# Later modulation units and passes, small rows ahead of x, and more scale columns on TensorE in a one-layer transformer kernel

## The reference

```python
mod = silu(c) @ w_ada + b_ada                       # (1024) @ (1024, 6*1024)
sh1, sc1, g1, sh2, sc2, g2 = split(mod, 6)
h = rmsnorm(x, pre_mix_gain) * (1 + sc1) + sh1
y = token_mixer(h, ...)                             # h @ w_in (1024 x 3072), 4 differential
                                                    # and 8 MoBA heads, @ w_out
x = x + g1 * rmsnorm(y, post_mix_gain)
h = rmsnorm(x, pre_ffn_gain) * (1 + sc2) + sh2
y = hier_moe(h, ...)                                # 32 SwiGLU experts, 2 per token
x = x + g2 * rmsnorm(y, post_ffn_gain)
```

## Time and profile before

| what | value |
|---|---|
| median of 3 runs | 747.18 us (745.7 to 748.9) |
| the profiled execution's own time | 747.51 us |
| its span in the profile | 745.8 us |
| PE busy | 713.7 us (96%) |
| DVE busy | 643.8 us (86%) |
| ACT busy | 523.9 us (70%) |
| POOL busy | 148.4 us (20%) |
| HBM read and written | 334 GB/s over the span |

### The profile page before, as it was taken

How to read it: one execution, slowest core, us unless ns; L and a number is a source line. 1 busy time by engine, 2 the same in 40 slices (tenths; PEclk the granted TensorE clock), 3 DMA queues, 4 the chain that set the end, 5 groups by cost and what they waited for, 6 DMA issues and landing times.

```text
span 745.8 us, 13100 instructions
## 1 busy us (share of the span) xinstructions
PE 713.7 (96%) x4839; PEld 567.5 (76%) x4839; DVE 643.8 (86%) x575; ACT 523.9 (70%) x571; POOL 148.4 (20%) x190
## 2 busy tenths in 40 slices
PE   4999799998899999999999999999999999999994
PEld 4785685545778888888888888888888888888873
DVE  4635776756779999999999999999999999999995
ACT  4011233644568888888888888888888888888883
POOL 5502100040141112221111122211111122111000
PEclk9999899999699999999999999999999999999998
DMA  8999998823398999999999999999999999999901
GB/s 304 347 379 391 386 403 343 314 83 145 137 322 311 380 382 377 381 383 375 375 377 374 386 368 384 383 378 371 380 374 382 383 377 380 377 382 377 356 1 60
DMA packets 102154, 249.20 MB, mean 334 GB/s; under 512 B 5266, under 2 KB 5326, under 8 KB 100078
## 3 DMA queue, kind: packets, MB, share of 16 engines
q1 hardware_dynamic: 99648, 244.33, 88.3%
q0 software_dynamic: 1008, 3.31, 1.2%
q10 hardware_dynamic: 1470, 1.22, 0.5%
HBM read 247.78 MB, written 1.07 MB: 334 GB/s over the span
## 4 chain that ended last, share of the span: by engine, by line
PE 90%; DVE 4%; DMA 3%; ACT 1%; issue 1%; ACTq 0%; DVEq 0%; SPq 0%
PE PS L1485 48%; PE PS L1473 8%; PE PS L1434 6%; PE PS L1191 4%; PE PS L1452 4%; PE PS L1443 4%; PE PS L1352 3%; PE PS L1235 3%; PE PS L1247 2%; DVE MOD L784 1%; DMA W<-in_w_in_dram 1%; DMA PT<-in_pre_mix_gain_dram 1%; DMA W<-in_w_ada_dram 1%; PE PS L1146 1%; PE PS L1264 1%
## 5 line engine op out<-in xcount | busy, mean ns | idle before, releaser
L1033 DVE TENSOR_TENSOR WL<-W,WH 128x2048 fp32r<-128x2048 f32 x185 | 417.5, 2296 | 9.1 <-ACT WH L688 9.1
L688 ACT CAST WH<-W 128x2048 fp32r<-128x2048 f32 x185 | 346.6, 1907 | 0.0
L1485 PE MATMUL PS<-WH,XT 128*128 128x512 f32 x512 | 142.5, 400 | 1.4 <-DVE XT L1052 1.4
L1485 PE MATMUL PS<-WL,XT 128*128 128x512 f32 x508 | 138.2, 393 | 0.0
L1485 PEld LDWEIGHTS PS<-WL,XT 128*128 128x128 f32 x508 | 95.3, 188 | 22.4
L1485 PEld LDWEIGHTS PS<-WH,XT 128*128 128x128 f32 x512 | 93.7, 188 | 21.3 <-DVE XT L1052 1.5
L457 POOL COPY cur<-PG 128x2 f32 (+1 forms) x31 | 5.7, 184 | 369.7 <-PE PS L1463 369.4
L1485 PE MATMUL PS<-WH,HT 128*128 128x512 f32 x248 | 69.6, 402 | 1.6 <-DVE HT L1064 1.6
L1485 PE MATMUL PS<-WL,HT 128*128 128x512 f32 x248 | 67.7, 395 | 0.0
L469 POOL CAST cur<-PG 128x6 bf16 (+1 forms) x31 | 58.5, 1887 | 0.0
L1485 PEld LDWEIGHTS PS<-WH,HT 128*128 128x128 f32 x248 | 44.3, 188 | 16.4 <-issue 8.0
(11 more groups left out here) (227 smaller groups left out, 887.4 us busy)
## 6 DMA issues: line engine op xcount, KB each, us to landing
W<-in_w_gate_dram SPq DMA_DIRECT2D x64, 1024.0 KB, 8.1
W<-in_w_down_dram SPq DMA_DIRECT2D x64, 1024.0 KB, 6.3
W<-in_w_up_dram SPq DMA_DIRECT2D x63, 1024.0 KB, 9.5
W<-in_w_ada_dram SPq DMA_DIRECT2D x16, 1024.0 KB, 7.7
W<-in_w_in_dram SPq DMA_DIRECT2D x12, 1024.0 KB, 8.4
W<-in_w_ada_dram SPq DMA_DIRECT2D x16, 512.0 KB, 5.8
W<-in_w_out_dram SPq DMA_DIRECT2D x4, 1024.0 KB, 8.0
toe<-line_dram POOLq DMA_DIRECT2D x1, 1536.0 KB, 12.2
```

The lines of the kernel that those rows point to most:

```text
L688: nc.scalar.copy(WH[(UPE * odd + u) % SPLITS][:], source).then_inc(hi_ready, 1)
L1033: nc.vector.tensor_tensor(low, source, WH[(UPE * odd + u) % SPLITS][:].bitcast(f32), ALU.subtract).then_inc(lo_ready, 1)
L1485: last = nc.tensor.matmul(PS[:, bank, :], lhsT, w[:, q * 512:(q + 1) * 512], start=begin, stop=end)
```

## The change

Six edits. (1) The order of the units: 3, 2, 3 and 8 `ada` units stand between and behind the `win` pairs in place of 4, 3, 4 and 5, so each `win` pair comes earlier; the `wout` units come in the order 2, 3, 0, 1. (2) DVE runs passes 0 and 1 ahead of the lambda sums and 2 and 3 behind them, instead of six passes behind them; then one pass in each of g = 0 to 3, two in each of g = 4 to 6, one in g = 7 and one behind. (3) ACT issues the small rows of gain, scale and shift ahead of x. (4) ON_TENSOR has four rows, k = 6, 7 too, so DVE has two passes fewer and PE 16 records more. (5) The shift columns go to two PSUM banks, two columns each; ACT copies one pair for itself, DVE the other; the two clears stand behind `shift_columns(0)`. (6) POOL's gain and router loads wait for w_in's unit (5, 1), and `sum_part(4)` and `sum_part(5)` each stand behind one more `project_out`.

```diff
-    between = (4, 3, 4, 5)
+    between = (3, 2, 3, 8)
...
-    return units + [("wout", u, 0) for u in range(4)]
+    return units + [("wout", u, 0) for u in (2, 3, 0, 1)]
...
-        ON_TENSOR = (2, 3)
-        FIRST_DONE = {(1, 0): 2, (1, 1): 6, (0, 0): 10, (0, 1): 15, (1, 2): 19, (1, 3): 23, (0, 2): 27, (0, 3): 32}
+        ON_TENSOR = (2, 3, 6, 7)
+        FIRST_DONE = {(1, 0): 2, (1, 1): 4, (0, 0): 8, (0, 1): 13, (1, 2): 17, (1, 3): 21, (0, 2): 25, (0, 3): 30}
...
-            pool.wait_ge(unit_in[slot_of(UNIT_AT["win", 3, 1])], 16 * uses_of(UNIT_AT["win", 3, 1]))
+            pool.wait_ge(unit_in[slot_of(UNIT_AT["win", 5, 1])], 16 * uses_of(UNIT_AT["win", 5, 1]))
...
                 act.dma_start(cR, c.rearrange("b (k p) -> (b k) p", p=P)).then_inc(c_in, 16)
-                for t in range(TT):
-                    act.dma_start(X[:, t, :], x[0, t * P:(t + 1) * P, :]).then_inc(x_in[t], 16)
                 act.dma_start(gainR, pre_mix_gain.rearrange("b (k p) -> (b k) p", p=P)).then_inc(pre_gain_in, 16)
                 act.dma_start(scaleR, b_ada[:, D:2 * D].rearrange("b (k p) -> (b k) p", p=P)).then_inc(ada_b_in, 16)
                 act.dma_start(shiftR, b_ada[:, 0:D].rearrange("b (k p) -> (b k) p", p=P)).then_inc(ada_b_in, 16)
+                for t in range(TT):
+                    act.dma_start(X[:, t, :], x[0, t * P:(t + 1) * P, :]).then_inc(x_in[t], 16)
...
                 act.wait_ge(scale_ready, half + 1)
+                act.wait_ge(shift_mm, 2 * half + 1)
+                nc.scalar.copy(shcol[:, 4 * half:4 * half + 2], PS[:, 3, 0:2]).then_inc(shift_ready, 1)
                 act.wait_ge(shift_ready, half + 1)
...
-                dve.wait_ge(shift_mm, half + 1)
-                nc.vector.tensor_copy(shcol[:, four], PS[:, 3, 0:4]).then_inc(shift_ready, 1)
                 dve.wait_ge(xT_mm, 2 * TT)
-                dve.wait_ge(shift_ready, half + 1)
+                dve.wait_ge(shift_mm, 2 * half + 2)
+                link(nc.vector.tensor_copy(shcol[:, 4 * half + 2:4 * half + 4], PS[:, 2, 0:2]))
...
+            dve.wait_ge(ada_b_rest, 16)
+            for n in range(2):
+                ada(n)
             dve.wait_ge(lam_in, 64)
...
-            dve.wait_ge(ada_b_rest, 16)
-            for n in range(6):
+            for n in range(2, 4):
                 ada(n)
...
             for g in range(PAIRS):
                 scores(g)
-                ada(6 + g)
+                ada(4 + g + max(g - 4, 0))
+                if 4 <= g < PAIRS - 1:
+                    ada(5 + g + (g - 4))
                 probabilities(g)
-            ada(14)
             ada(15)
...
-                    at = UNIT_AT["first", 1, 0]
-                    pe.wait_ge(unit_in[at], 16)
                     for k in ON_TENSOR:
+                        at = UNIT_AT["first", 1, k // 4]
+                        pe.wait_ge(unit_in[at], 16)
...
-                nc.tensor.matmul(PS[:, 3, 0:4], shiftR, ident[0:DC, 4 * half:4 * half + 4], start=True, stop=True)
+                for chunk in range(2):
+                    at = 4 * half + 2 * chunk
+                    nc.tensor.matmul(PS[:, 3 - chunk, 0:2], shiftR, ident[0:DC, at:at + 2], start=True, stop=True)
                 for chunk in range(2):
                     pe.wait_ge(first_used, FIRST_DONE[0, 2 * half + 1] - 1 + chunk)
-                    for col in (2 * chunk, 2 * chunk + 1):
-                        last = add_rows(PS[:, 3, col:col + 1], 0, 4 * half + col)
-                last.then_inc(shift_mm, 1)
+                    for col in range(2):
+                        last = add_rows(PS[:, 3 - chunk, col:col + 1], 0, 4 * half + 2 * chunk + col)
+                    last.then_inc(shift_mm, 1)
...
             scale_columns(0)
-            pe.wait_ge(bank_zero, 1)
-            pe.wait_ge(gcol_ready, 1)
-            clear(0)
-            clear(1)
             for t in range(TT):
...
             shift_columns(0)
+            pe.wait_ge(bank_zero, 1)
+            pe.wait_ge(gcol_ready, 1)
+            clear(0)
+            clear(1)
...
             transpose_probabilities(7)
-            sum_part(4)
             values_out(5)
             project_out(1, [5], False, False)
+            sum_part(4)
             weigh_values(7)
-            sum_part(5)
             values_out(6)
             project_out(1, [6], False, False)
+            sum_part(5)
             spread_inverse(0)
```

More of the change, by code:

```diff
@@ L1155, in scale_columns @@
                     pe.wait_ge(c_silu, 1)
-                    at = UNIT_AT["first", 1, 0]
-                    pe.wait_ge(unit_in[at], 16)
                     for k in ON_TENSOR:
+                        at = UNIT_AT["first", 1, k // 4]
+                        pe.wait_ge(unit_in[at], 16)
                         for col in range(4):
-                            nc.tensor.matmul(PS[:, 2, col:col + 1], W[at][:, k * HALF + col * P:k * HALF + (col + 1) * P], cS[:, k:k + 1],
+                            nc.tensor.matmul(PS[:, 2, col:col + 1], W[at][:, k % 4 * HALF + col * P:k % 4 * HALF + (col + 1) * P], cS[:, k:k + 1],
                                              start=False, stop=True, skip_group_check=True)
```

## The result

The changed kernel's median is 740.92 us (740.76 to 742.1, 5 runs), beside 745.7 us (744.43 to 748.9, 5 runs) of the kernel before on the same chip: ratio 0.9935, 95% interval 0.9908 to 0.9962. Timed again beside other runs of the kernel before it had 740.33 us, ratio 0.9914 (0.9893 to 0.9935). That is 4.8 and 6.9 us. Of the 2 us, 1.5 are not the change: beside the changed kernel the kernel before has 745.7 us, and the forecast started from its 747.18. The gain itself was forecast at 4.3 us. The profiled execution took 740.76 us with a span of 739.0 us (before 747.51 and 745.8 us).

A forecast was written before the change was run, and what follows sets the result against it. The expert stage was taken as fixed, so time ahead of it counts fully. A 5.3 us lead, start's +0.6 included, less 1.0 given back makes -4.3: 747.51 to 743.2, median 0.33 lower, 742.9 us; range 740.4 to 746.0.

The forecast's parts named there:

- What bounds the kernel: Expert stage: PE full, fixed time from the first gather, so time gained ahead moves the end one for one.
- The first scores and the clock: `scores(0)`, released by ACT's exponential, at 75.2 not 78.15 us (-3.0); PE's stand falls from 4.15 to 0.6 us.
- The clock's part: Second projection round: no half clock without the long stand, 9.35 becomes 6.91 us, -2.4; rival, clock still falls, chance 0.12.
- Passes in pairs: DVE, g = 4 to 6: first pair covered with 0.14 us left; rival, PE stands for DVE, 749.5 us, chance 0.06.
- The copy behind `exps(7)`: `sum_part(3)` waits for ACT's copy until 137.4 us, giving back 1.0 of the 5.3 us lead.
- The start: Edits 3, 4, 5, up to 58 us: unit 1 lands no earlier, 16 new PE records cost time, +0.6 us (0 to 1.5).
- The rival of an earlier rise: Start: 16 more PE records raise the clock earlier, -2.3 us and no start loss, 740.0 us, chance 0.11.

The follow-up runs named there:

- once more: The changed kernel, nothing altered, timed and profiled again in the next group of runs: 740.33 us, ratio 0.9914.
- The two runs with the filled stand: Kernel before with 14 unread matmuls in PE's stand behind `score(1)`: 749.51 us; the same with POOL's gain and router loads late: 743.8 us.
- stand filled: Kernel before with 14 matmuls, result unread, put ahead of the first transposes of the probabilities, loads left early: 749.51 us, ratio 1.003.
- two scale rows: The changed kernel with ON_TENSOR back at (2, 3), edit 4 undone: 740.79 us, ratio 0.9913.
- all but the passes: The changed kernel with edit 2 undone, six DVE passes again behind the lambda sums: 750.25 us, ratio 1.0049.
- the start alone: The kernel before with edits 3, 4 and 5 only: 745.65 us, ratio 0.9979.

## Why the prediction was right, point by point

The times of PE in the table are those of the timeline; the chain has some of them 0.2 us later.

| step | forecast | changed kernel | once more |
|---|---|---|---|
| unit 1 landed | 12.95 us | 11.61 | 11.89 |
| `half_projection` starts | 25.7 us | 23.08 | 24.12 |
| projection 2 starts (57.98 before) | 58.6 us | 55.93 | 57.69 |
| first scores | 75.2 us | 72.56 | 74.32 |
| from projection 2 to the first scores | 16.6 us | 16.63 | 16.63 |
| stand of PE for the first probabilities | 0.6 us | 0.62 | 0.63 |
| second round | 6.9 us | 6.91 | 6.91 |
| `sum_part(3)` | 137.4 us | 134.43 | 136.21 |
| the 48 records | 152.5 us | 149.31 | 151.09 |

**What bounds the kernel: held.** PE is busy for all of the 100 us from 300 us on after the change as well, and SP stands for PE 170 times, 380.1 us. The time gained ahead of the experts came out at the end, 6.8 of 7.5 us in the profile.

**The first scores and the clock: held, the way from projection 2 to the scores to a tenth of a us.** The exponential releases the scores, in the changed kernel and with edit 2 alone. What was needed for it was edit 2. The clock's part went with the stand and was somewhat larger than forecast: PE's lead over the kernel before grows from 5.59 us at the first transposes (84.85 and 79.26) to 8.39 at the second (95.89 and 87.50), 2.8 us and not 2.4, since the first transposes had run at the lower level too (0.90 us, now 0.55). The changed kernel's second profile has 3.82 and 6.61 us, the same 2.8. The two runs with the filled stand show that this term holds only together with units that are in time. I had this as one sentence ("its unit lands earlier than before, since POOL's gain rows no longer run beside it"), and the 1.003 of the first of them is what it is worth when it fails. The reason in it was not what counted: with edit 2 alone POOL's loads stay early, and the pass of the second head pair, at 81.07 us, has no wait, because it is pass 5 there and not pass 7.

**Passes in pairs: held, with little room.** 0.14 us was forecast and 0.05 us measured at the fifth head pair. This rival did not come: the view of PE's waits shows no stand for DVE from the second head pair to the eighth.

**The copy behind `exps(7)`: held.** PE's lead is 8.33 us before `sum_part(3)`, where PE then stands 1.23 us, and 7.5 us at the 48 records. In between the kernel before had stood 0.39 us for its last pass at `sum_part(4)`, and the changed one doesn't. So 0.9 of 8.4 us were given back, where 1.0 was forecast; in the second profile 0.9 of 6.6.

**The start: the step that failed.** It was forecast at +0.6 us, from "x and the first units share the same transfers, so their order doesn't bring unit 1 earlier". Their order does: the eight profiles with the small rows first have unit 1 by 11.47 to 11.89 us, the six with x first by 12.01 to 12.97 us. Of the 1.6 us between the forecast 25.7 us and the 24.12 us of the second profile, 1.06 us are this. The cost of the 16 new records was right (3.57 us, forecast 3.50), and with x first the changed kernel does start late. What the start as a whole is worth is best read at projection 2 over all profiles: the five with the kernel before's start have 55.92, 55.93, 55.97, 55.98 and 57.98 us, the five with the changed start (not counting those with a part of it) 54.88, 55.92, 55.93, 55.99 and 57.69 us. The medians are 55.97 and 55.93 us. So the start's term is 0, not +0.6 us, and the profile that the forecast started from was the latest of its five there, by 2 us.

**The first scores were undersized by that late start.** In the kernel before, a lead at projection 2 does not reach the first scores whole, because they wait for the sixth pass's unit. From projection 2 to the first scores the kernel before took 20.2 us. With the stand filled, which is the same code up to there, it was 21.1 us (55.97 to 77.09), and with the small rows first 20.9 (56.35 to 77.27). The changed kernel takes 16.63 us both times. So from a start in the common place the first scores come 4.5 us earlier (77.09 and 72.56), where the forecast has 3.6 without its start's term. The profile with the small rows alone has the rest of the way in the old manner:

```profile
77.27 1.02 DVE S L862 x2
...
156.01 20.61 PE PS L1352 x48
```

Its 48 records start 6.7 us behind the changed kernel's 149.31, 6.3 with the 0.4 us between their starts taken off. The forecast's terms with 0 for the start, 2.8 for the clock and 0.9 given back make 5.5 us, and with 4.5 at the first scores 6.4; measured were 4.8 and 6.9. That the forecast of 4.3 lies within half a us of the first of them is in part luck, since its errors at the start and in the gain at the first scores do not cancel but stand on the same side.

**The rival of an earlier rise** gave the side of the miss by luck more than by its mechanism: the changed kernel's profile has 16 records between 25 and 29 us, where the earlier trace rows has 10. But the 16 more records on PE are not its cause, since the four further profiles with the kernel before's own start, without them, are at projection 2 by 55.98 us too.

**What stays open.** Behind the 48 records the changed kernel's first profile loses 0.7 us and its second gains 1.0 us on the kernel before. The clock's half-speed stretches in the router and in the first rounds of the experts lie in other places in each, as the row from 207 to 212 us shows for the first. The busy time by stretch of the second has this instead:

```profile
207.00:212.00 5.00, 3.44 (x21) 2.80 (x19) 4.97 (x6) 5.00 (x5) 3.40 (x4) 1.00 1.04 350
```

Whether the change moves these places on average, or they only fall differently in each execution, was not separated, and neither was the 2 us between the two measured gains: the kernel before had 745.7 us in one group of runs and 747.27 in the other, the changed kernel 740.92 and 740.33.

## What to carry to other kernels

Ask of a wait for a transfer first whether its consumer may stand later in its own engine's order: two passes moved behind the engine's next deadline gave here what a new order of transfers did not. All the other edits without this one made the kernel slower (1.0049). A stand of PE that is followed by half clock costs twice (4.15 us and then 2.8 here), but filling it helps only when what comes next is in time; look for the wait that the slow stretch hides. And where the order of small and large loads at the start decides what lands when, read several profiles: one execution's place of the clock's rise was worth 2 us here, more than three times the term that was being estimated, and a lead ahead of a wait for a transfer is not worth its full size behind it.

## What the runs showed of the hardware

**Where the granted clock rises at the start moves between executions of one kernel.** The stretch from 25 to 29 us of the changed kernel's second profile, with the columns of the earlier trace rows:

```profile
25.00:29.00 4.00, 4.00 (x11) 3.13 (x10) 3.34 (x6) 0.00 (x0) 4.00 (x6) 1.00 1.04 373
```

It has 11 records where the first profile of the same code has 16 (above), so it is at the lower level; its clock column has 1.00 only because it has no entry yet, as in the earlier trace rows. Its 32 records of the dense run take 9.35 us where the first has 8.83. It is the same for the kernel before's start: its profile reaches projection 2 at 57.98 us, four others with this start by 55.98 us. The Trainium skill (TensorE: Matmul & The Clock Gate, Part 1) says that the chip's look at activity isn't tied to the kernel's start and that the count of cold matmuls varies between runs of one kernel. The traces agree, with a size of 2 us here.

**Short stands and the fall.** I had taken the price of a fall to be one size. The runs have it in more sizes. Each row is PE's stand ahead of the probabilities' transposes, and the projection of 32 records right behind them:

| kernel | stand | 32 records |
|---|---|---|
| changed (both profiles), and six others | 0.28 to 0.66 us | 6.91 us |
| before, stand filled (first head pair) | 1.29 us | 6.91 us |
| changed, two scale rows | 1.96 us | 8.13 us |
| before, stand filled (second head pair) | 2.20 us | 8.60 us |
| all but the passes | 3.88 us | 8.39 us |
| before | 4.15 us | 9.35 us |
| the start alone | 4.60 us | 7.93 us |
| before, small rows first | 4.61 us | 9.42 us |

The 32 records are counted from the end of PE's records right before them. Up to 1.29 us no round is longer, and from 1.96 us on each is, by 1.0 to 2.5 us; the length of the stand doesn't order them, as two stands of 4.6 us with 7.93 and 9.42 us show.

The busy time by stretch with two scale rows shows that the clock, and not a wait, is what lengthens the round:

```profile
80.00:85.00 5.00, 4.54 (x15) 3.87 (x16) 4.92 (x9) 2.34 (x9) 0.00 (x0) 0.66 1.00 404
```

This execution lost 1.2 us there, and yet its kernel's ratio is that of the changed one (0.9913): one profile fixes little.

**Small transfers and large ones in one queue.** The row of pre_mix_gain, issued behind x, landed at 10.28 us; ahead of x its first use is at 4.83 us. And x, issued behind three more small transfers, lets SP's unit 1 land earlier by some 0.7 us (the middle of either set).
